# A hybrid decoder step in one launch: down products on two sets of banks in turn, the last expert in one block of four units, rows and three weight pieces requested sooner

## What is computed

```python
def _moe(h, router_g, router_e, w1, w3, w2):
    g_prob = softmax(hf @ router_g); g_val, g_idx = top_k(g_prob, 1)      # one of 4 groups
    e_logits = (hf @ router_e)...[the group's 8 experts]
    e_val, e_idx = top_k(softmax(e_logits), 2)                            # two experts of the group
    gate = g_val * e_val / sum(e_val)
    ...
    def block(args):
        xb = h[tok]
        return (silu(xb @ w1[e]) * (xb @ w3[e])) @ w2[e]
    y[slot_tok] += out * slot_w
```

## Time and profile before

| | us |
|---|---|
| runs | 1465.8, 1466.87, 1469.98 |
| profiled execution, device time | 1473.97 |
| its span, first to last instruction | 1472.1 |
| routing stage, from its first instruction | 846.7 to 880.1 |
| expert stage, TensorE's first product to its last | 894.7 to 1422.5 |
| last stage, TensorE's first product to the end of the span | 1433.35 to 1472.1 |
| blocks in the expert stage (transpositions of x) | 33, of which the last has one unit |

### The profile page before, as it was taken

The page is one execution under the profiler, slowest core; times in us unless marked ns, Lnnn a source line. Parts: engine busy times, 40 slices in busy tenths (PEclk is TensorE's granted clock), DMA queues, the critical chain, the costliest instruction groups (busy, mean ns, idle before and its releaser), DMA issues. The chain is left out here.

```text
span 1472.1 us, 33644 instructions
## 1 busy us (share of the span) xinstructions
PE 1368.9 (93%) x13661; PEld 960.7 (65%) x13661; DVE 671.2 (46%) x1362; ACT 309.4 (21%) x843; POOL 566.1 (38%) x452
## 2 busy tenths in 40 slices
PE   8999999998998999999999858999999989999864
PEld 4678888865566668887777534666666766666641
DVE  4757787842325567666667471112112111111127
ACT  1311011113113444443443100011001001100015
POOL 4212423402223235543334012445545544445435
PEclk9999999999998999999999979999999999999987
DMA  6334333244136232213321199999999999999936
GB/s 250 89 97 99 76 78 102 61 121 160 47 110 245 90 100 80 86 66 115 115 94 44 72 396 376 388 399 399 396 396 404 395 395 398 395 395 395 392 87 237
DMA packets 129606, 318.04 MB, mean 216 GB/s; under 512 B 48120, under 2 KB 86512, under 8 KB 103672
## 3 DMA queue, kind: packets, MB, share of 16 engines
q1 hardware_dynamic: 109720, 294.35, 53.3%
q0 software_dynamic: 18656, 18.15, 5.7%
q10 hardware_dynamic: 1152, 4.52, 0.8%
HBM read 277.05 MB, written 47.74 MB: 221 GB/s over the span
## 5 line engine op out<-in xcount | busy, mean ns | idle before, releaser
L2660 PE MATMUL bank<-sb_arena 128*32 128x256 f32 x6144 | 341.5, 381 | 12.2 <-DVE sb_arena L2768 5.7
L2660 PEld LDWEIGHTS bank<-sb_arena 128*32 128x32 f32 x6144 | 222.9, 111 | 125.4 <-issue 13.2
L515 PE MATMUL bank<-sb_arena 128*128 128x276 f32 x1008 | 235.0, 395 | 0.0
L2631 POOL DMA_INDIRECT d_acc<-sb_arena,sb_oidx x96 | 152.1, 1584 | 194.0 <-ACT sb_arena L2726 166.0
L515 PEld LDWEIGHTS bank<-sb_arena 128*128 128x128 f32 x1008 | 191.0, 190 | 44.0
L2676 PE MATMUL bank<-sb_arena 128*32 128x256 f32 x3072 | 172.9, 379 | 7.7 <-ACT sb_arena L2726 7.6
L2676 PEld LDWEIGHTS bank<-sb_arena 128*32 128x32 f32 x3072 | 110.6, 110 | 66.4 <-ACT sb_arena L2726 9.9
L2624 POOL DMA_INDIRECT sb_arena<-d_x,sb_idx x99 | 102.6, 1037 | 109.4 <-DVE sb_idx L2754 51.8
L2773 DVE TENSOR_SCALAR sb_oidx<-sb_slot 128x3 int32 x32 | 5.6, 174 | 286.1 <-DMA d_acc<-sb_arena,sb_oidx 285.7
L2726 ACT ACTIVATE sb_arena<-bank,sb_arena 128x256 f32<-128x256 f32 x96 | 38.5, 472 | 397.1 <-DVE sb_arena L2774 387.7
L1281 PE MATMUL bank<-sb_arena 128*128 128x512 f32 (+1 forms) x256 | 119.7, 596 | 0.0
(11 more groups left out here) (420 smaller groups left out, 1842.5 us busy)
## 6 DMA issues: line engine op xcount, KB each, us to landing
sb_arena<-w SPq DMA_DIRECT2D x192, 1024.0 KB, 28.1
sb_arena<-w_conv SPq DMA_DIRECT2D x28, 512.0 KB, 4.8
sb_arena<-d_conv SPq DMA_DIRECT2D x7, 1792.0 KB, 7.3
d_conv<-sb_arena SPq DMA_DIRECT2D x22, 512.0 KB, 3.3
sb_arena<-d_gam SPq DMA_DIRECT2D x8, 768.0 KB, 5.2
d_x<-sb_arena SPq DMA_DIRECT2D x9, 512.0 KB, 2.6
sb_arena<-xT ACTq DMA_DIRECT2D x8, 552.0 KB, 9.3
sb_arena<-w_out SPq DMA_DIRECT2D x8, 512.0 KB, 7.9
```

Of the source, the lines that this page charges most:

```text
L515: last = e.matmul(bank[at + t][:, 0:HT // 2], weights[:, k, :], x[:, k, HT // 2 * t:HT // 2 * t + HT // 2], start=(k == 0), stop=(k == HK ...
L2631: e.indirect_dma_start(rows_out, bass.IndirectOffsetOnAxis(ap=oidx[:, r:r + 1], axis=0), eo[:, r, :], None, bounds_check=LAST_ROW, oob_is_ ...
L2660: mm = e.matmul(bank[UPB + r][j * CG:(j + 1) * CG, 0:2 * P], xgT[:, 2 * q + k, r * CG:(r + 1) * CG], w13[s][q][:, k, j, :], start=(q == 0 ...
```

## The change

- **Banks in turn.** `down` writes to banks 4 and 5 for even blocks and 6 and 7 for odd ones, two of its three units sharing a bank (`out_of`). It waits for the evictions of block n-2. It does units 0 and 1 for all four parts of the sum, then unit 2. TensorE's loop body is six blocks, and five more are unrolled behind it; ScalarE's loop body is two.
- **Order on VectorE.** `h_flip(b)` stands ahead of `mark(b-1)`.
- **Last expert.** An expert with 97 to 128 tokens goes last as one block of four units (128 rows): the fourth unit is gathered on its own (`xg_end`), up products go to banks 0 to 3, and the down product is eight products of 128x128 stationary and 128x512 moving. The blocks are one fewer. Ahead of it TensorE does down of the block before. The routing code is rewritten for this and no longer builds the old part block.
- **Rows.** SyncE requests the last stage's rows at the end of the expert stage, once the scatters have landed, into the buffer of w13 of the third set and the first of w2 behind it (`rows_at`).
- **Three pieces.** w13 q = 0, 1, 2 of expert 0 are requested in the chunk loop at i = 2 instead of in the routing stage, into the place of `ch` and `spread`, which are moved to the front of the arena.

```diff
+E2 = E - 2
+UP_SET = E2 % NSET
+DOWN_SET = (E2 - 1) % NSET
+END_SET = E1 % NSET
...
                 for i in range(1, NTT + 2):
+                    if i == 2:
+                        for c in range(4):
+                            e.wait_ge(S[f"ch_st{c}"], 32)
+                        e.wait_ge(S["ss_ps"], 8)
+                        for q in range(EARLY):
+                            e.dma_start(early[q], a["w13"][0, q]).then_inc(W["w13" + "abcd"[q] + "0"], 16)
                     if i + 1 < NTT:
                         load_gam(i + 1)
...
-                    for q in range(4):
+                    for q in range(EARLY if s == 0 else 0, 4):
...
+                e.tensor_scalar(spans, iota[:, 0:E], -float(BLK), float(BLK * (E - 1)), ALU.mult, ALU.add)
+                step(e.tensor_scalar(col[1], col[7], -float(BLK * EPG), float(BLK * (EPG * EPG + EPG)), ALU.mult, ALU.add))
+                for j in range(2):
+                    e.scalar_tensor_tensor(first_at[:, j, :], col[8 + j], -float(BLK), col[1], ALU.mult, ALU.add)
...
+                step(e.scalar_tensor_tensor(over, count, float(WIDE), over, ALU.is_le, ALU.mult))
+                step(e.tensor_reduce(wide_of, over, AX, ALU.max))
+                step(e.tensor_scalar(star, number, wide_of[:, 0:1], None, ALU.is_equal))
...
+                step(e.tensor_scalar(xblk, rowi[:], 1.0, -1.0, ALU.max, ALU.add))
+                step(e.scalar_tensor_tensor(xblk, star, 0.0, xblk, ALU.is_equal, ALU.mult))
+                step(e.tensor_tensor_scan(until, ones[:, 0:E], xblk, 0.0, ALU.mult, ALU.add))
+                step(e.tensor_tensor(extra, until, xblk, ALU.subtract))
+                step(e.scalar_tensor_tensor(extra, star, float(REST - E), extra, ALU.mult, ALU.max))
+                step(e.scalar_tensor_tensor(shift, extra, float(BLK), spans, ALU.mult, ALU.add))
...
+                e.tensor_tensor(cmp_, bc1(row[6][0:1], 1, NX, E), bc(turn, 1, NX, E), ALU.is_le).then_inc(S["r_v"], 1)
+                e.tensor_scalar(is_end, turn, total, None, ALU.is_equal)
...
+                step(e.tensor_reduce(oexp, cmp_, AX, ALU.add))
...
+        OUT = [4, 6]
+        SIX = 2 * NSET
+        def out_of(side, r):
+            return bank[OUT[side] + r % 2][:, 256 * (r // 2):256 * (r // 2 + 1)]
...
+                before = of(source, e.snap(last - 1), 0, E - 1)
+                ex_end = of(source, last, 0, E - 1)
+                for h in range(2):
+                    e.wait_ge(S["e_out"], 2 * (E2 - NSET) + h + 1)
+                    later2(h, UP_SET, before)
+                for q in range(4):
+                    e.wait_ge(S["e_up"], 4 * (E1 - NSET) + q + 1)
+                    later13(q, END_SET, ex_end)
                 for h in range(2):
                     e.wait_ge(S["e_out"], 2 * (E1 - NSET) + h + 1)
-                    later2(h, UP_SET, ex_end)
+                    later2(h, END_SET, ex_end)
+                e.wait_ge(S["e_st"], 48 * last + 16)
+                for t in range(NTT):
+                    n = m_of(t)
+                    e.dma_start(rows[t][0:n], a["d_acc"][row_of(t):row_of(t) + n, :]).then_inc(LOADED[t], 16)
...
-                def down(n, s, load):
+                def down(n, s, load, side, evicted):
                     e.wait_ge(S["e_hT"], n + 1)
                     for r in range(NR):
-                        e.wait_ge(S[f"e_eo{r}"], n + 3)
...
+                        e.wait_ge(S[f"e_eo{r}"], evicted)
+                    for units in ((0, 1), (2,)):
+                        for h in range(2):
+                            if units == (0, 1):
+                                e.wait_ge(W["w2" + "ab"[h] + str(s)], 16 * load)
+                            for k in range(2):
+                                c = 2 * h + k
+                                for r in units:
+                                    for j in range(4):
+                                        mm = e.matmul(out_of(side, r)[j * CG:(j + 1) * CG], hT[:, c, r * CG:(r + 1) * CG], w2[s][h][:, k, j * 256:(j + 1) * 256],
+                                                      start=(c == 0), stop=(c == 3))
+                            if units == (2,):
+                                mm.then_inc(S["e_out"], 1)
+                        if units == (0, 1):
+                            mm.then_inc(S["e_down2"], 1)
...
+                with nc.Fori(0, (E2 - 2) // SIX, engines=bass.OrderedEngineSet([e.engine]), hint_back_edge=True) as i:
+                    for j in range(SIX):
...
+                for n in range((E2 - 2) // SIX * SIX + 1, E2):
+                    up(n, n % NSET, n // NSET + 1 + (AHEAD_UP if n % NSET == UP_SET else 0))
+                    down(n - 1, (n - 1) % NSET, (n - 1) // NSET + 1 + (AHEAD_DOWN if (n - 1) % NSET == DOWN_SET else 0), (n - 1) % 2, n + 1)
+                with e.Fori(E2, last) as b:
                     up(b, UP_SET, b)
-                    down(e.snap(b - 1), DOWN_SET, b)
+                    down(e.snap(b - 1), DOWN_SET, b, (E2 - 1) % 2, e.snap(b + 2))
+                down(e.snap(last - 1), UP_SET, E2 // NSET + 1, E2 % 2, E2 + 2)
                 e.wait_ge(S["e_xT"], last + 1)
                 e.wait_ge(S["e_hm"], last)
                 for q in range(4):
+                    e.wait_ge(W["w13" + "abcd"[q] + str(END_SET)], 16 * (E1 // NSET + 1))
                     for k in range(2):
...
+                        for r in range(NR + 1):
+                            for j in range(4):
+                                mm = e.matmul(bank[UPB + r][j * CG:(j + 1) * CG, 0:2 * P], xgT[:, 2 * q + k, r * CG:(r + 1) * CG], w13[END_SET][q][:, k, j, :],
+                                              start=(q == 0 and k == 0), stop=(q == 3 and k == 1))
                     mm.then_inc(S["e_up"], 1)
...
+                        for d in range(2):
+                            mm = e.matmul(bank[UPB + d][:, :], hT[:, c, :], w2[END_SET][h][:, k, d * 512:(d + 1) * 512], start=(c == 0), stop=(c == 3))
+                    mm.then_inc(S["e_out"], 1)
...
                     gate(b)
+                    h_flip(b)
                     mark(e.snap(b - 1))
-                    h_flip(b)
...
+                e.activation(eo_last[:, 0:512], bank[UPB][:, :], ACT.Copy, scale=tok_last[:, 1:2])
...
+                e.tensor_scalar(eo_last[:, 512:D], bank[UPB + 1][:, :], tok_last[:, 1:2], None, ALU.mult)
```

More of the change, by code:

```diff
@@ L2368, in _ @@
                 e.memset(xg, 0.0)
+                e.memset(xg_end, 0.0)
                 e.memset(eo, 0.0)
@@ L2446, in _ @@
                 step(e.tensor_reduce(dest[:, 1, :], oh32[1], AX, ALU.add))
+                step(e.tensor_tensor(dest, dest, first_at, ALU.add))
                 flat = dest.rearrange("p j t -> p (j t)")
@@ L2502, in _ @@
-                e.tensor_scalar(order[0:1, NBMAX:NBMAX + 4], iota[0:1, 0:4], 0.0, float(NBMAX), ALU.mult, ALU.add)
-                for k in range(2):
-                    e.tensor_scalar(ends[0:1, k:k + 1], total, float(E - 1 - k), None, ALU.add)
-                step(e.tensor_scalar(table[0:1, 0:1], total, float(E), None, ALU.add))
-                later = iota[0:1, 0:NOVER]
-                far13, near13, far2, near2 = [A(1, NOVER) for _ in range(4)]
-                e.tensor_scalar(far13, later, 12.0, float(4 * E1 - 11), ALU.mult, ALU.add)
@@ L2680, in _ @@
-                idle_products(e, bank[7][:, :], 8)
-                up(0, 0, 1, first=True)
-                with nc.Fori(0, (E - 2) // NSET, engines=bass.OrderedEngineSet([e.engine]), hint_back_edge=True) as i:
-                    for j in range(NSET):
-                        before, s = e.snap(NSET * i + j), (j + 1) % NSET
-                        up(e.snap(NSET * i + (j + 1)), s, e.snap(i + (2 if s == 0 else 1) + (AHEAD if s == UP_SET else 0)))
-                        down(before, j, e.snap(i + 1 + (AHEAD if j == DOWN_SET else 0)))
@@ L2713, in _, with tanh @@
                 last = last_block(e)
-                def tanh(n, first=False):
+                def tanh(n, first=False, units=NR):
                     e.wait_ge(S["e_up"], 4 * n + 4)
```

269 lines of the change are left out of this document (121 added, 148 removed).

## The result

| | before | after |
|---|---|---|
| median | 1466.62 us (4 runs, 1465.8 to 1469.98) | 1486.93 us (4 runs, 1483.79 to 1491.39) |
| ratio, 95% interval | | 1.0136 [1.0104, 1.0169] |
| span of the profiled execution | 1472.1 us | 1489.6 us |
| block 0's up product to last stage's first product | 538.66 us | 564.48 us |

The changed kernel is slower by 1.4%, 20 us. The forecast was 1453.5, the range ended at 1461.5.

A forecast was written before the change was run, and what follows sets the result against it. The stream of weights, 17.4 us a block, was taken as the bound. Span 1472.1 - 13.7 - 0.3 = 1458.1; with 0.6 kept back, 13.4 less than the median shown, 1466.87, gave 1453.5 us; range 1446.5 to 1461.5.

The forecast's parts named there:

- The bound: End of the expert stage: the stream of weights, 17.4 us a block, is the bound; TensorE's 15.7 us of waits are slack.
- Price 0: Scatter chain in the expert stage: 16 to 17.4 us a block, at or under the stream's, so it costs nothing.
- Fresh code in a row costs nothing: TensorE's instruction supply: straight code costs 0, as the first pass from 923.51 on shows no gap.
- 0.6 us for more instruction loads: Held back in the sum for TensorE's longer code, leaving a gain of 13.4 us.
- in the full stream: Scatter whose last issue ends at 1389.94: landing seen 10.7 us later, against 1.3 with the stream empty.
- Rival (a): TensorE's loop: every pass jumps to code that is gone; 32 us of stalls, 19 late, 1472.5; chance 0.11.
- The 13 us of cover: TensorE before block 31: without waits done at 1377.7, by the stream 1391.1, so 13 us of stalls are covered.
- Part 1: Banks in turn, flip before mark: price 0 while the stream is the bound; -7.6 us if it were not.
- part 4: Last block of four units: up 31 from 1391.1 takes 13.7 us; its evictions end at 1417.7.
- Part 2: Three weight pieces requested in the chunk loop: cost 0, at most 1; gain 0.5 us, at most 2.7.
- Part 3: Shorter list of blocks in VectorE's routing chain: 1.7 us earlier, between 0 and 3.
- Parts 4 to 6: Wide last block, stage end and sooner rows: last stage starts at 1419.6, 13.7 us earlier; rows bring 0.3 more.

The follow-up runs named there:

- e6_before_two: The kernel before with the third scatter of each block left out, a third of the expert output missing: 1459.81 us, ratio 0.9934.
- e8_early_gates: e4_three_alt with a block's gates copied before the wait on the landed scatter and its indices after, nothing left out: 1457.13 us, ratio 0.9918.
- e4_three_alt: The kernel after with TensorE's loop over three blocks, banks in turn as far as that allows (sides 0, 1, 0): 1462.2 us, ratio 0.9954.
- e1_straight: The kernel after with TensorE's six-block loop written out as straight code, no jump back: 1486.54 us, ratio 1.0123.
- e3_before_six: The kernel before with TensorE's loop over six blocks instead of three, nothing else: 1497.61 us, ratio 1.0188.
- e13_before_alt: The kernel before with only banks in turn (sides 0, 1, 0, three-block loop) and the flip ahead of mark: 1470.27 us, ratio 1.0003.
- e14_no_early: e4_three_alt with all 18 first weight pieces requested at the head of the routing, none in the chunk loop: 1462.92 us, ratio 0.9956.
- e2_one_set: The kernel after with one set of output banks, old order of products, marks ahead of flips and a three-block loop: 1473.65 us, ratio 1.0018.

## Why the prediction was wrong, step by step

**The bound.** "So at the end of the stage the stream is the bound" was half right. In before the stream does run without a hole and with 17.4 us a block. But the scatter chain, 16.3 us a turn, came last: an issue of 1.9 us less in each turn gave 10 us (e6_before_two, a part of it perhaps by the lighter stream), and 0.45 less, with nothing left out, gave 5 (e8_early_gates against e4_three_alt). The forecast compared paces, 16 to 17.4 against 17.4, and concluded "at or under the stream's. Price 0". A pace is not a lateness. The stream starts with three blocks of buffers in hand and may lose 1.1 us a block to the chain for most of the stage; the chain has one block of output banks.

**The failed step: what fetched code costs.** The forecast asked of instruction supply only whether TensorE has gaps: "Fresh code in a row costs nothing: there is no gap in the first pass from 923.51 on." Its sum kept back 0.6 us for more instruction loads; the runs show 27. There is no gap, and yet it costs. The price was paid by the scatters' landings, 1.2 us each, which show on VectorE. e1_straight shows it in full with code in a row and without a jump. The rows were there: the 10.7 us landing of the earlier trace rows came right behind the loop's exit of the earlier trace rows, while code was being fetched (two packets of q8 from 1386 to 1402), and was booked as the value "in the full stream". The steady value is 9.1, in a stream just as full. From three-block to six-block body the ratios rise by 0.0182, 27 us (e4_three_alt to after), and by 0.0188, 28 us (before to e3_before_six).

**Rival (a)** had the signs right (q8 packets in every pass, gaps behind them) and the jump nearly (7.3 forecast, 8 measured), and the wrong mechanism for the time. Its chance of 0.11 leaned on the hint; the hint saves 3.6 of 11.7 us and didn't keep the body of 3456 on the engine. The Trainium skill, Runtime: NRT & Kernel Launch, Instruction fetch mechanics, gives TensorE's memory 2048 instructions and says that a taken branch to code outside "the current 2-page window" stalls the engine: for the body of 3456 the trace agrees (gaps of 1.19 and 4.18 us at the first jump). Pages of 256 instructions, as the section has them, would make that window 512, and there the trace differs: the body of 1728 was jumped through without one packet of q8 from 955 to 1380. The same section says that the fetching of code in a row is mostly hidden, and names the stalls of branches as one reason why kernels prefer full unrolling. Here the straight kernel took as long as the one with jumps: had the stalls been the cost, it would have come out near 1466 (the estimate for e1_straight), and it came out at 1487.

**The 13 us of cover.** Measured with the chain out of the way, some 17 of 25 us of stalls are covered, give or take 4. Right in kind, and about right in size. In the real kernel the cover is the chain, and the chain was the thing that got longer.

**Part 1, price 0:** the number was right (1.0003) for a reason that wasn't. It was to cost nothing because the stream is the bound. But the chain was, and its turn stayed 16.3: e13_before_alt still waits 8.4 us for evictions and 7.9 for the gate, where before waits 7.6 and 5.7. That is luck. What the forecast missed besides is that part 4 depends on part 1: 9 us.

**Part 2, gain 0.5:** nothing against it, but e14_no_early can't tell 0.5 from 0. **Part 3, 1.7 (0 to 3) us earlier:** from VectorE's first reduction of the routing to block 0's product it is 47.94 before (846.75 to 894.69) and 45.00 after (842.56 to 887.56), so 2.9, at the end of its bounds; the other 4 us by which block 0 begins sooner lie in the chunk loop and are no effect of the change, for in e3_before_six, whose loop is unchanged, the routing begins at 841.50.

**Parts 4 to 6.** Up 31 14.0 (13.7 forecast), gap 3.0 (3.3), down 31 10.05 and 8.8 in e4_three_alt (8.9), from its end to the last stage 2.2 (2.6). The tail's arithmetic holds to 1 us. What fails is its start. In e4_three_alt, where the tail is the same and the loop short, the last stage begins 534.8 us after block 0, forecast some 527; these 8 us are late before up 31. There the chain sets the time, and the straight code behind the loop lengthens its last four turns to 17.3 to 18.7. So of the 33 us between forecast and result, 27 are the six-block body, and the other 6 are lateness of the chain, which the forecast had at price 0. How these 6 divide was not separated: one part may be a second stall of GpSimd, told below, which e2_one_set, e4_three_alt and e14_no_early have near 1345 and which before and e13_before_alt don't have.

## What to carry to other kernels

When a longer loop body makes an engine fetch its code in every pass (here 3456 instructions; 1728 stayed), look past that engine: the packets go through the DMA engines, and a chain of small dependent transfers pays, here 1.2 us a turn, 27 us in all, with or without jumps. For each resource that recurs once per block ask how late it may be at the end of the stage, not only how fast it runs. And take a latency for a forecast from the steady stretch, after looking at what else was in the queues beside the row.

## What the runs showed of the hardware that was not expected

- A 16 KB packet of code in some 7 us raised the landing of indirect scatters from 9.1 to 10.3 us while from 960 to 1300 the DMA engines moved 394 against 397 GB/s: next to nothing of bandwidth, 13% of latency. In q8 a packet takes 0.9% of 16 engines over 425 us and 61 packets, 1.0 us each, near the 1.2 that a landing grew. Whether one such packet in the scatter's way is the whole of it stays open.
- Single transfers of 12 KB, four a block, cost far more: 64 us against e4_three_alt by the ratios, since the stream of weights fell behind.
- GpSimd stalls for 8 to 9 us between two gathers, for nothing that the profile names: once in before (until 1200.42), twice in after (until 1144.49 and 1373.77, 13 blocks apart; GpSimd's timeline, after):

```profile
1363.36 1.08 POOL L2646 DMA_INDIRECT sb_arena<-d_x,sb_idx  x1 [0.30 <-issue]
1373.77 1.04 POOL L2646 DMA_INDIRECT sb_arena<-d_x,sb_idx  x1 [9.33 <-issue]
```

The up product of block 29, behind it, is the one at 1383.66 with 5.90 us of idle time. In e1_straight two up products are 21.5 and 21.8 us after the last instead of some 17.4, one behind each stall; behind the first, two blocks at 15.54 make most of it good, behind the second the stage ends before that. A second stall of this kind falls inside the stage in after, e1_straight, e2_one_set, e4_three_alt and e14_no_early, and in before, e3_before_six and e13_before_alt it doesn't. What it costs, and its cause, were not tried.
